# Depth part 0 of four SwiGLU layers by the seven-product scheme, with its sums by transfer and joined operand splits

## What is computed

```python
D_MODEL, D_FF = 1024, 2816

def swiglu(h, w_in, w_out):
    gate, up = jnp.split(h @ w_in, 2, axis=-1)
    return (jax.nn.silu(gate) * up) @ w_out

x = x + 0.5 * swiglu(rms_norm(x, ffn1_norm[layer]), ffn1_w_in[layer], ffn1_w_out[layer])
x = x + mixer(rms_norm(x, mix_norm[layer]))
x = x + 0.5 * swiglu(rms_norm(x, ffn2_norm[layer]), ffn2_w_in[layer], ffn2_w_out[layer])
```

## Time and profile before

| | us |
|---|---|
| median of 3 runs | 2257.74 (2256.77 to 2259.69) |
| profiled execution, own time | 2259.44 |
| its span, first to last instruction | 2257.6 |
| mean granted TensorE clock | 0.999 |

### The profile page before, as it was taken

How to read it: one execution, slowest core, us unless ns; L and a number is a source line. 1 busy time by engine, 2 the same in 40 slices (tenths; PEclk the granted TensorE clock), 3 DMA queues, 4 the chain that set the end, 5 groups by cost and what they waited for, 6 DMA issues and landing times.

```text
span 2257.6 us, 46708 instructions
## 1 busy us (share of the span) xinstructions
PE 2212.9 (98%) x18627; PEld 2162.0 (96%) x18627; DVE 1705.9 (76%) x2960; ACT 1168.6 (52%) x2229; POOL 452.5 (20%) x353
## 2 busy tenths in 40 slices
PE   9999999999999999999999999999989999999998
PEld 8999999998989999999999999999988899999998
DVE  7868887567675958887967888689755657778884
ACT  5546665333323536665545666454444644556663
POOL 2111112000151201111301111244033632011111
PEclk9999999999999999999999999999999999999999
DMA  4478984222202458986258888322310002488891
GB/s 137 123 174 185 201 199 127 96 89 93 77 11 94 108 146 181 211 192 155 76 141 185 190 195 188 106 75 76 94 53 2 30 29 94 114 196 193 186 205 62
DMA packets 372311, 287.19 MB, mean 127 GB/s; under 512 B 9562, under 2 KB 365406, under 8 KB 372089
## 3 DMA queue, kind: packets, MB, share of 16 engines
q1 hardware_dynamic: 267502, 227.79, 33.5%
q0 software_dynamic: 92288, 48.24, 16.7%
q10 hardware_dynamic: 12306, 8.18, 1.3%
HBM read 278.07 MB, written 6.10 MB: 126 GB/s over the span
## 4 chain that ended last, share of the span: by engine, by line
PE 53%; DVE 8%; DMA 5%; issue 2%; ACT 2%; POOL 1%; ACTq 0%; SPq 0%; DVEq 0%; POOLq 0%
PE ps L945 23%; PE ps L846 6%; PE ps L692 6%; PE ps L1013 5%; PE ps L989 4%; DMA wsum_added<-ffn_w_out 3%; DMA wsum_added<-ffn_w_in 2%; DVE cacc L2708 2%; PE ps L1047 2%; PE ps L3609 1%; DVE wl L677 1%; DVE pre L2697 1%; ACT cacc L2777 1%; DVE wl L837 0%; PE ps L3454 0%
## 5 line engine op out<-in xcount | busy, mean ns | idle before, releaser
L945 PE MATMUL ps<-bop,wh 128*128 128x272 f32 x4032 | 761.0, 288 | 0.7 <-ACT comb L1382 0.7
L945 PEld LDWEIGHTS ps<-bop,wh 128*128 128x128 f32 x4032 | 633.1, 188 | 1.5 <-issue 0.7
L945 PE MATMUL ps<-bop,wl 128*128 128x272 f32 x2016 | 582.2, 289 | 0.0
L831 ACT ACTIVATE wh<-raw 128x512 fp32r<-128x512 f32 (+1 forms) x456 | 262.5, 591 | 238.5 <-PE ps L945 90.1
L945 PEld LDWEIGHTS ps<-bop,wl 128*128 128x128 f32 x2016 | 378.8, 188 | 0.0
L837 DVE TENSOR_TENSOR wl<-raw,wh 128x512 fp32r<-128x512 f32 (+1 forms) x456 | 291.4, 657 | 58.2 <-ACT wh L831 53.5
L1382 ACT ACTIVATE comb<-ps 128x272 f32<-128x272 f32 x416 | 164.9, 396 | 202.7 <-PE ps L945 160.6
L989 PE MATMUL ps<-hop,wh 128*128 128x272 f32 x1344 | 253.4, 288 | 7.2 <-ACT comb L1382 7.2
L1259 POOL DMA_DIRECT2D wsum_added<-ffn_w_in x64 | 99.6, 1556 | 670.0 <-DMA wsum_added<-ffn_w_in 612.4
L692 PE MATMUL ps<-xh,wh 128*128 128x288 f32 (+1 forms) x1056 | 225.1, 294 | 3.5 <-DVE wl L677 3.1
L989 PEld LDWEIGHTS ps<-hop,wh 128*128 128x128 f32 x1344 | 210.6, 188 | 8.7 <-issue 8.7
(11 more groups left out here) (521 smaller groups left out, 4328.2 us busy)
## 6 DMA issues: line engine op xcount, KB each, us to landing
raw<-ffn_w_in SPq DMA_DIRECT2D x88, 1024.0 KB, 5.6
raw<-ffn_w_out SPq DMA_DIRECT2D x48, 768.0 KB, 5.1
wsum_added<-ffn_w_in SPq DMA_DIRECT2D x128, 256.0 KB, 6.1
wsum_added<-ffn_w_in POOLq DMA_DIRECT2D x64, 512.0 KB, 8.8
raw<-odd_w_in SPq DMA_DIRECT2D x16, 1024.0 KB, 5.5
raw<-even_w_in SPq DMA_DIRECT2D x14, 1024.0 KB, 4.9
wsum_added<-ffn_w_out SPq DMA_DIRECT2D x64, 192.0 KB, 7.4
wsum_added<-ffn_w_out POOLq DMA_DIRECT2D x32, 384.0 KB, 8.9
```

Source lines behind the costliest of these rows:

```text
L831: nc.scalar.activation(entry(op)[0][:, 0:block_nk(u), :], op_source(u, i), ACT.Copy).then_inc(op_hi.sem, 1)
L945: ins = nc.tensor.matmul(ps[:, bank, 0:TH], w[:, k, :], bop[:, r, k, :], start=i in S_OPEN and k == 0 and a == 0, stop=k == KH - 1 and a = ...
```

## The change

1. `SCHEME` becomes (0, 1, 2): part 0's 16 output units (4 in each FFN) become seven-product ones, and pairs 0, 1 and 2 go through `hidden_turns` and `hop`. The second product of the lead pairs is stored negated (`lead_product`), as the scheme wants it. An FFN then has 30 blocks.
2. Blocks 0 and 1 of each FFN get sums 0 and 3 by transfers too. Their loads go into SyncE's queue behind the raw load of unit 3 and wait for the first product of unit 1; the accumulates go into GpSimd's queue between the two pairs of gate products.
3. Where operands 2 and 3, or 5 and 6, of the next unit lie side by side in one ring buffer, they are split by one ScalarE and one VectorE instruction each, at the later one's place.
4. In the odd mixer, ScalarE runs a one-element Exp behind the last gate, and TensorE's wait for the last unit norms moves into the first delta block.

```diff
-SCHEME = (1, 2)
+SCHEME = (0, 1, 2)
...
     def sum_wait(eng, u, k):
-        if not early_block(u) and k in (0, 3):
-            eng.wait_ge(sum_added.sem, sum_added.at(16 * late_before(u) + 16))
+        if k in (0, 3):
+            eng.wait_ge(sum_added.sem, sum_added.at(16 * u.block + 16))
         else:
...
+            eng.wait_ge(sum_made.sem, sum_made.at(2 * u.block + k))
...
+    def as_pair(u, i):
+
+        return u.n_ops == 7 and i in (2, 5) and op_entry[u.op + i] % 4 < 3
...
+    def pair_split_hi(act, u, i):
+        if i == 2:
+            sum_wait(act, u, 2)
+        for op in (u.op + i, u.op + i + 1):
+            if op in op_first:
+                act.wait_ge(unit_done.sem, unit_done.at(op_first[op]))
+            elif op_prev[op] is not None:
+                act.wait_ge(op_used.sem, op_used.at(op_prev[op] + 1))
+        nc.scalar.activation(pair_entry(wh, u, i), pair_source(u, i), ACT.Copy).then_inc(op_hi.sem, 2)
+
+    def pair_split_lo(dve, u, i):
+        dve.wait_ge(op_hi.sem, op_hi.at(u.op + i + 2))
+        nc.vector.tensor_tensor(pair_entry(wl, u, i), pair_source(u, i), pair_entry(wh, u, i).bitcast(F32),
+                                ALU.subtract).then_inc(op_lo.sem, 2)
...
         gate(0, 0)
         gate(0, 1)
+        ffn_sums_pool(pool, f, w_in, w_out, ffns[f][2 * LEAD_PAIRS:2 * LEAD_PAIRS + 2])
         gate(1, 0)
         gate(1, 1)
+        ffn_sums_pool(pool, f, w_in, w_out, ffns[f][2 * LEAD_PAIRS + 2:])
...
-        if at < 3:
+        if at < 0:
+            sp.wait_ge(op_used.sem, op_used.at(ffns[u.f][1].op + 1))
+        elif at < 3:
             sp.wait_ge(op_used.sem, op_used.at(ffns[u.f][3].op + 4))
...
         v = ffns[u.f][u.at + 1]
-        if v.n_ops == 7:
+        if as_pair(v, place):
+            return
+        if v.n_ops == 7 and place and as_pair(v, place - 1):
+            (pair_split_hi if split is op_split_hi else pair_split_lo)(eng, v, place - 1)
+        elif v.n_ops == 7:
             split(eng, v, place)
...
             sp.dma_start(dst, src).then_inc(raw_loaded[slot].sem, 16)
+            if u.at == 2 * LEAD_PAIRS - 1:
+                for b in range(2):
+                    sums_first(sp, blocks[first_block[f] + b], w_in, w_out)
...
         gate_silu(31)
+        nc.scalar.activation(touch[:, 0:1], eps[:, 0:1], ACT.Exp)
...
             pe.wait_ge(gt.sem, gt.at(8))
+            if dl.b == 0 and g == 1:
+                pe.wait_ge(l2_done.sem, l2_done.at(15))
...
         pe.wait_ge(proj_out.sem, proj_out.at(I_ODD + 32))
-        pe.wait_ge(l2_done.sem, l2_done.at(16))
```

More of the change, by code:

```diff
@@ L1080, in hidden_hi @@
     def hidden_hi(act, u, step):
-        minus = step == 1 and u.pair >= LEAD_PAIRS
+        minus = step == 1 and (u.pair >= LEAD_PAIRS or by_blocks(u))
         if not by_blocks(u):
@@ L1209, in weight_sum_dve @@
             return
-        early = early_block(u)
-        if k == 0 and early:
+        if k == 1:
+            sum_wait(dve, u, 0)
             dve.wait_ge(raw_loaded[u.raw % 2].sem, raw_loaded[u.raw % 2].at(8 * (u.raw - u.raw % 2) + 16))
[L1213 to L1217, removed]
+            if not early_block(u):
                 dve.wait_ge(op_lo.sem, op_lo.at(blocks[u.block - 1].op + 4))
@@ L1243, in sums_first, with ffn_sums_pool @@
             sp.dma_start(out[:, c, :, :], src[:, :, c * P:(c + 1) * P]).then_inc(sum_loaded.sem, 16)
-    def ffn_sums_pool(pool, f, w_in, w_out):
-        for u in ffns[f]:
-            if u.n_ops != 7 or early_block(u):
+    def ffn_sums_pool(pool, f, w_in, w_out, units):
+        for u in units:
+            if u.n_ops != 7:
                 continue
@@ L1254, in ffn_sums_pool @@
                 src = w_in.rearrange("(k p) n -> p k n", p=P)[:, :, n0:n0 + P]
[L1255 to L1258, removed]
+            whole = wsum_first[u.block - first_block[f]][:, 0:2, :, :] if early_block(u) else wsum_added[late_before(u) % 3][:]
+            out = whole.rearrange("p a k n -> p (a k) n")[:, 0:2 * block_nk(u), :]
+            pool.wait_ge(sum_loaded.sem, sum_loaded.at(32 * u.block + 32))
+            if u.block:
+                pool.wait_ge(sum_added.sem, sum_added.at(16 * u.block))
             pool.dma_start(out, src, accum_op=ALU.add).then_inc(sum_added.sem, 16)
@@ L1266, in lead_product @@
             dve.wait_ge(hl_ready.sem, hl_ready.at(hidden_before(u.f, 0) + 2))
-        nc.vector.tensor_tensor(two(sq[c][:]), halves(2 + c), two(gbuf[c][:]), ALU.mult).then_inc(h_made.sem, 1)
+        if c and by_blocks(u):
+            nc.vector.scalar_tensor_tensor(out=two(sq[c][:]), in0=halves(2 + c), scalar=-1.0, in1=two(gbuf[c][:]),
+                                           op0=ALU.mult, op1=ALU.mult).then_inc(h_made.sem, 1)
+        else:
+            nc.vector.tensor_tensor(two(sq[c][:]), halves(2 + c), two(gbuf[c][:]), ALU.mult).then_inc(h_made.sem, 1)
     def ffn_lead_dve(dve, f, n):
```

53 lines of the change are left out of this document (31 added, 22 removed).

## The result

| | us |
|---|---|
| before, median of 4 runs | 2257.26 (2256.01 to 2259.69) |
| after, median of 4 runs | 2274.94 (2271.00 to 2277.52) |
| ratio | 1.0070, 95% interval 1.0058 to 1.0082 |
| profiled execution of after: own time, span, granted clock | 2277.52, 2275.7, 0.995 |

The change made the kernel 17.7 us slower; 2249.3 was forecast, with 2242.5 to 2257.0 as the range.

The account below looks back on a forecast made before the run. TensorE, busy in 98% of the span, was taken as the bound, with GpSimd's serial accumulates setting output parts' ends. -18.0 + 9.2 + 1.6 - 1.2 = -8.4 us gave 2249.3 against 2257.74, range 2242.5 to 2257.

Parts of the forecast that it names:

- TensorE's own gain: Part 0's output units: 63 matmuls a unit instead of 72, all on the path, -18.0 us.
- The accumulates of part 0: Part 0's end: shorter lead before GpSimd's serial accumulates makes TensorE wait, +9.2 us (bounds 3.6 and 13.2).
- rival A: Part 0: accumulates hidden, waits 0.9 or less as in other parts; 2241.3, or 2243 with joins' cost; chance 0.17.
- a changed lead: Sign in the profile: if part 0's lead over its accumulates changes, the prediction is wrong.
- VectorE, "inside the 9.2": Units 4 to 6: 34.8 us of VectorE work in 31.64; delays counted inside the accumulates' 9.2, not added.
- The joined splits: Pairs split by one instruction: later ends delay raw loads and shorten parts' leads, +1.6 us (-0.8 to +5).
- The saving by joins: VectorE: 0.07 us for each of 176 joins, 12 us over the kernel, none on the path.
- The odd layer: Odd mixer: Exp's table load runs beside the DMA issues, -1.2 us (0 to -1.3).
- C: Units 4 to 6: VectorE's backlog delays raw and sum loads and holds the accumulate chain; +7 us, 2265; chance 0.07.
- loads that land just before the issue: Sign in part 0's accumulates that the slower rival's mechanism, late sum loads, is at work.
- B: Part 0 and joins: full accumulate cadence, joins cost 4 us; -1.4 us, 2253 to 2258; chance 0.26.
- D: Joined splits do nothing at all; counted within the forecast, no chance of its own.

Follow-up runs that it names:

- x1: The changed kernel without the joined splits; 2249.98 us, ratio to before 0.9967.
- x8: x1 with ScalarE's bank copies moved ahead of hidden copies and of the fifth operand's split; 2257.27 us, ratio to before 0.9995.
- x6: The changed kernel with only operands 5 and 6 (raw weights of the right half) joined, 2 and 3 split singly; 2259.23 us, ratio to before 1.0002.
- x5: The changed kernel with only operands 2 and 3 (weight sums) joined, 5 and 6 split singly; 2269.82 us, ratio to before 1.0043.
- x12: x1 without the odd mixer's two edits (early Exp, moved wait for the last unit norms); 2249.53 us, ratio to before 0.9966.
- x4: The kernel before with the seven-product scheme on part 0 alone: no early transfers, joins or early Exp; 2254.19 us, ratio to before 0.9986.
- x7: The changed kernel with every split single, a pair's two one behind the other at the later one's place; 2260.18 us, ratio to before 1.0002.

## Why the prediction was wrong, by its own steps

- **TensorE's own gain, -18.0.** Right. 144 matmuls went. Part 0 fell by 15.5 us in x1 (144.3 to 128.8), which is 18.0 less 2.6 of waits.
- **The accumulates of part 0, +9.2.** The place was wrong, and the size came out near it by luck. The cadence was right: in x1 the five of FFN 3 took 1184.90 - 1137.71 = 47.19 us by GpSimd's timeline:

```profile
1137.71 1.45 POOL L1291 DMA_DIRECT2D wsum_added<-ffn_w_out  x1 [8.05 <-DMA wsum_added<-ffn_w_in]
...
1184.90 1.56 POOL L1291 DMA_DIRECT2D wsum_added<-ffn_w_in  x1 [7.17 <-DMA wsum_added<-ffn_w_in]
```

  The lead was not 18.32 but 20.02 (part 0 starts at 1157.73), since units 4 to 6 took longer. So the transfers cost 2.6 us over all four parts, which is rival A's mechanism, and the delays ahead of them 9.9 (137.1 - 127.2), together 12.5 for my 9.2; the 5.4 us that parts 1 and 2 gave back (below) covered that and more. I had written that such delays only move part 0 towards a chain that sets its end. In x8 this holds: it took 3.2 out of units 4 to 6, the lead of each part 0 fell by 1.14 and part 0 gave 5.1 back. In after it doesn't: units 4 to 6 took 8.2 longer than in x1, the lead grew by 2.43, and the sixth issue still came 1.05 later, since five intervals took 50.9 us in place of 47.4. I had read the earlier trace rows as if GpSimd waited for the accumulate before and nothing else. It also waits for the block's own loads, and the profile gives both by the same tile name. By the landing times in the traces the loads came last in 16 of the 40 issues behind the first in before's parts 1 and 2, in 10 of 20 in x1's part 0 and in 14 of 20 in after's, there by up to 5.2 us. So delays of TensorE and of the splits reach the chain too. The forecast named a changed lead as a sign that it would be wrong; the sign came, in x1 without the loss.
- **VectorE, "inside the 9.2".** Right without joins: in x1 VectorE was busy 32.28 of the 34.24 us that units 4 to 6 of FFN 3 took; I had 34.8 of work for it. With joins it stood idle in them, and the 9.2 had no more room: lengthening them by another 8.2 us (137.1 to 145.3) did not shorten part 0's waits, it even went with longer ones (128.8 to 134.5: four times 1.05 by the later sixth issue, 1.5 by the clock, below).
- **The joined splits, +1.6 (-0.8 to +5). This is the step that failed:** 16 us on before, 25 on the new kernel. "What a join costs is order: both halves wait for the second one's place" was right, but I followed it only at the unit's end (the slot's next raw load, the part's lead), and priced that at 0.2 a part; it costs 10.6 us over the twelve parts by x6's ledger, 9.2 by its median. I did not follow the pair 2 and 3 in ScalarE's queue at all, whose next entries are the copies that TensorE waits for: this pair costs 19.8 us (x5). Nor did I ask what the first half does while the second's source isn't there: it fills a wait. The earlier trace rows show VectorE at 57.52 of 63.54 there, so the sums arrive with little to spare, and in the unit shown above the instruction bound to the second of them was on the path.
- **The saving by joins, 0.07 each on VectorE.** About right by starts: 1149.72 - 1148.58 = 1.14 against twice 0.60, so 0.06. The page's busy time fell by 21.1 us from x1 (1781.1) to after (1760.0) for 176 instructions, 0.12 each by durations, which overlap. The Trainium skill ("VectorE: DVE Perf Modes", the TRN2 errata) would have 0.157 each, 28 us. By either it bought nothing.
- **The odd layer, -1.2.** Right in the trace (1.3 us here, 1.6 between the means of the stretches compared under x12), too small to be seen in the time. ScalarE in after:

```profile
1677.02 0.66 ACT L2827 ACTIVATE dgate<-dgate 128x544 f32<-128x544 f32 x1 [5.54 <-DVE dgate L2765]
1677.69 1.28 ACT L2866 ACT_TABLE_LOAD   x1
...
1679.73 0.45 ACTq L3569 DMA_DIRECT2D causal_s<-c_causal_s  x1
1680.23 1.28 ACT L3260 ACTIVATE dW<-dW,ngamc 128x128 f32<-128x128 f32 x4 [1.04 <-DVE kcoef L3352]
```

  The table load runs beside the DMA issues. From the last DMA issue to the first Exp: 1667.86 - 1666.08 = 1.78 before, 1680.23 - 1679.73 = 0.50 after, 1.28 less. The load follows the gate at once (1677.02 + 0.66), so the drain that the Trainium skill ("ScalarE: Activation LUTs", "What ACT_TABLE_LOAD costs") adds isn't seen here either.
- **Not forecast:** parts 1 and 2 are 5.4 us shorter in x1 than before, and as much in x4, so it comes with the scheme on part 0. By the table of issues, the sixth issue comes 0.64 us sooner in each of the eight parts (26.88 against 27.52), 5.1 of the 5.4. Why it does I haven't found out. It was luck for the forecast: without it the rest of the change would have gained some 3 us and not 8.2.
- **Rivals.** C named a slower end, units 4 to 6 as its place, and late loads of sums as the way. Its sign, loads that land just before the issue, is in after's part 0 (14 of 20), and in 16 of 40 issues before; but it was to come from the scheme's work for VectorE, and x1, which has that work, is faster than before. What lengthened units 4 to 6 was the joins, in ScalarE's queue. B had joins that cost, at 4 us. D said the joins do nothing.

## What to carry to other kernels

Joining two instructions saves a fixed cost and ties both to the later of two sources, to the longer duration and to one completion. Before joining, list for each half when its source is ready, what its engine does while it waits for the second, and what stands behind it in the queue; where an engine waits for the second source anyway, the first half is free and the join can be a loss, however idle that engine is (here ScalarE was busy 53% of the span). And a saving ahead of a stretch whose end a serial chain sets is given back there: x8 took 3 us out of one and lost 5 in the next. But look first whether the chain waits only for itself: here it also waited for loads that hang on the kernel's other work.

## What the runs showed of the hardware

TensorE's granted clock fell to half after some of the new waits. The windows of after around the wait in part 0 of FFN 1, where TensorE stood 1.81 us from 135.78 on after a gapless stretch (column before the DMA share: the clock):

```profile
134.00:137.90 3.90, 2.09 (x17) 1.90 (x16) 1.37 (x3) 1.37 (x4) 0.70 (x1) 1.00 1.12 302
137.90:141.30 3.40, 3.40 (x17) 3.40 (x16) 3.40 (x7) 1.61 (x4) 0.86 (x1) 0.50 1.16 240
141.30:144.70 3.40, 3.40 (x29) 3.40 (x28) 2.63 (x5) 2.09 (x3) 0.29 (x1) 1.00 0.63 78
```

In 3.40 us TensorE starts 17 matmuls at 0.50 (1.2 GHz) and 29 at 1.00 (2.4 GHz): 12 lost, 1.5 us, almost as much as the wait itself. It happened again at 335.9, behind a wait of 2.16 in the last part of FFN 1, but not behind the waits of 1.95 and 1.76 that ended at 2006.06 and 2103.61 (3.40 us from 2007.20 and from 2105.00 on start 29 matmuls each at 1.00), so a long wait doesn't always bring it. These two are the parts whose end came 6.52 and 6.66 us behind the sixth issue, where 5.1 is usual. Three more such parts, one in x6 and two in x7 (6.5 to 6.7), followed waits of 2.02, 3.05 and 1.79. It is a small part of the loss: the run of after at clock 1.000 took 2271.00, still 13.7 us more than before's median.
